# Two banded attentions: keys projected once per pair, the second half of the queries projected among the first attention units

## The reference

```
qkv = x @ w_qkv + b_qkv             # 16 query heads, 4 key and 4 value heads, 64 wide
# blocks of 128 queries; block n sees the keys of blocks n-1 and n
scores = einsum('bnqhgd,bnkhd->bnhgqk', q, kb) * 64 ** -0.5
scores = where(band and has_prev, scores, -inf)
probs = softmax(concatenate([scores, sink]))[..., :-1]
out = einsum('bnhgqk,bnkhd->bnqhgd', probs, vb) @ w_o + b_o
```

## Time and profile before

| | us |
|---|---|
| median of three runs | 4046.59 |
| lowest, highest | 4042.22, 4052.07 |
| the profiled execution, its own time | 4044.99 |
| its span in the trace | 4043.2 |
| PE busy | 3593.7 (89%) |
| DVE, ACT busy | 1854.7 (46%), 1375.2 (34%) |
| mean granted clock of PE | 0.914 |

### The profile page before, as it was taken

How to read it: one execution, slowest core, us unless ns; L and a number is a source line. 1 busy time by engine, 2 the same in 40 slices (tenths; PEclk the granted TensorE clock), 3 DMA queues, 4 the chain that set the end, 5 groups by cost and what they waited for, 6 DMA issues and landing times.

```text
span 4043.2 us, 47237 instructions
## 1 busy us (share of the span) xinstructions
PE 3593.7 (89%) x20284; PEld 2936.8 (73%) x20284; DVE 1854.7 (46%) x2920; ACT 1375.2 (34%) x2362; POOL 127.6 (3%) x167
## 2 busy tenths in 40 slices
PE   7988989885898989668798999997998999799898
PEld 6976979754697966367597987795555788656697
DVE  4524555404455544543455542553334555603476
ACT  3423444411344432110244432441342443312354
POOL 0000000000000000011000000001001000000000
PEclk9987999997899989676798997998999999899999
DMA  6542545435454523621454542541002233422253
GB/s 223 189 120 73 188 152 188 138 123 180 136 188 151 185 83 125 198 84 63 139 185 151 188 145 70 167 157 54 26 24 83 92 116 136 135 84 73 79 180 107
DMA packets 421534, 523.45 MB, mean 129 GB/s; under 512 B 53927, under 2 KB 363804, under 8 KB 421196
## 3 DMA queue, kind: packets, MB, share of 16 engines
q1 hardware_dynamic: 420524, 518.33, 39.3%
q0 software_dynamic: 800, 2.10, 0.2%
HBM read 518.29 MB, written 2.10 MB: 129 GB/s over the span
## 4 chain that ended last, share of the span: by engine, by line
PE 84%; DVE 9%; ACT 4%; POOL 2%; issue 1%; DMA 1%; SPq 0%; POOLq 0%; DVEq 0%; ACTq 0%
PE ps L184 17%; PE ps L185 17%; PE ps L186 16%; PE ps L176 15%; PE ps L194 3%; PE ps L272 3%; PE ps L947 3%; PE ps L404 1%; PE ps L1496 1%; PE ps L1123 1%; POOL small L453 1%; PE ps L2572 1%; PE ps L1266 1%; POOL junk L2308 1%; ACT junk L494 1%
## 5 line engine op out<-in xcount | busy, mean ns | idle before, releaser
L184 PE MATMUL ps<-a 128*128 128x256 f32 (+1 forms) x4488 | 1426.9, 318 | 53.8 <-DVE a L543 35.0
L185 PE MATMUL ps<-a 128*128 128x256 f32 (+1 forms) x4488 | 1423.9, 317 | 0.0
L186 PE MATMUL ps<-a 128*128 128x256 f32 (+1 forms) x4488 | 1420.8, 317 | 0.0
L184 PEld LDWEIGHTS ps<-a 128*128 128x128 f32 x4488 | 866.8, 193 | 116.6 <-issue 22.1
L186 PEld LDWEIGHTS ps<-a 128*128 128x128 f32 x4488 | 865.6, 193 | 54.4
L185 PEld LDWEIGHTS ps<-a 128*128 128x128 f32 x4488 | 867.0, 193 | 51.7
L674 DVE TENSOR_TENSOR a<-ring,a 128x1024 fp32r<-128x1024 f32 x594 | 693.6, 1222 | 371.1 <-ACT a L668 371.1
L668 ACT ACTIVATE a<-ring 128x1024 fp32r<-128x1024 f32 x594 | 585.9, 1048 | 280.7 <-PE ps L186 226.3
L765 ACT ACTIVATE tmp<-ps 128x256 f32<-128x256 f32 x176 | 67.6, 384 | 518.2 <-PE ps L186 518.2
L771 DVE TENSOR_TENSOR a<-tmp,ps 128x256 f32<-128x256 f32 x176 | 74.3, 422 | 309.4 <-ACT tmp L765 309.4
L176 PE MATMUL ps<-ring,xt 128*128 128x512 f32 (+1 forms) x512 | 207.4, 566 | 4.3 <-ACT xt L1057 2.9
(11 more groups left out here) (324 smaller groups left out, 3337.8 us busy)
## 6 DMA issues: line engine op xcount, KB each, us to landing
ring<-in_ffn_w_in_dram SPq DMA_DIRECT2D x220, 1024.0 KB, 7.3
ring<-in_ffn_w_out_dram SPq DMA_DIRECT2D x121, 1024.0 KB, 5.0
ring<-in_ada_w_dram SPq DMA_DIRECT2D x48, 1024.0 KB, 6.0
ring<-in_gla_w_in_dram SPq DMA_DIRECT2D x12, 1024.0 KB, 5.5
ring<-in_rwkv_w_rkv_dram SPq DMA_DIRECT2D x12, 1024.0 KB, 5.0
ring<-in_na_w_qkv_dram SPq DMA_DIRECT2D x12, 1024.0 KB, 5.1
ring<-in_swa_w_qkv_dram SPq DMA_DIRECT2D x10, 1024.0 KB, 5.1
ring<-in_swa_w_o_dram SPq DMA_DIRECT2D x8, 1024.0 KB, 5.0
```

What stands on the lines that cost most here:

```text
L184: pe.x.matmul(out, lh, rh, start=start and i == 0, stop=False)
L185: pe.x.matmul(out, lh, rl, start=False, stop=False)
L186: ins = pe.x.matmul(out, ll, rh, start=False, stop=stop and i == n - 1)
```

## The change

In both banded mixers:

- **Keys.** Two key blocks instead of four: block p holds key heads 2p and 2p+1, each once, from one 1 MB load. ACT evacuates each head with its bias into its own half of the partitions; the other half is filled by a DMA from SBUF to SBUF, four in all, issued by POOL and counted by a new semaphore `s_dup`. PE waits for all four before the first scores.
- **Order of the projections.** Keys, values, then query blocks 0 to 3, over banks 5, 6 and 7. Query blocks 4 to 7 are projected from the function `before`: PE computes block 3+i ahead of the scores of iteration i = 1 to 4, all into bank 5; ACT evacuates block 2+i ahead of its iteration i = 2 to 5. PE waits for the last of them ahead of iteration 6.
- **Order of the jobs.** First half of the heads for query blocks 0 and 1 (units 0, 1 and 2 to 5), then the second half (units 6, 7 and 8 to 11), since query blocks 4 to 7 hold the second half. The sinks' and the output's indices follow.
- **Transposes** use two banks (3 and 4) in turn here instead of three; the other attentions keep three.

```diff
 def pe_attention(...):                        # and the same in act_attention
-            if m >= 3:
-                pe.wait_ge(*s.act.at(tag, "pt", m - 3))
-            flips(K, pe, K.ps[:, 3 + m % 3, :], ...)
+            if m >= A.turns:
+                pe.wait_ge(*s.act.at(tag, "pt", m - A.turns))
+            flips(K, pe, K.ps[:, 3 + m % A.turns, :], ...)
 def swa_memory(K, tag, layer, j):
-    for t in range(2):
-        for half in range(2):
+    for half in range(2):
+        for t in range(2):
 def sp_swa(K, sp, M, f):
+    load_cols(K, sp, (tag, "k"), w, 1024, 256, 8, (s.pe, (tag, "k", 1)))
+    sp_projB(K, sp, (tag, "v"), w, 1280, 256, (0, 1))
     sp_projA(K, sp, (tag, "q"), w, 0, D)
-    for g0 in (0, 2):
-        c = K.w.take((tag, "k", g0), 4, (K.s.pe, (tag, "k", g0 + 1)))
...
-    sp_projB(K, sp, (tag, "v"), w, 1280, 256, (0, 1))
+def pe_swa_queries(K, pe, M, i, rot):
+    c = K.w[(tag, "q"), i // 2 * 256]
+    bank, freed = rot.take(s.act, tag, "q", "out", i)
+    pe.wait_ge(*c.landed)
+    pe.wait_ge(*freed)
+    mms(pe, bank[:, 0:T], [...8 pairs...]).then_inc(*s.pe.up((tag, "q"), i))
 def pe_swa(K, pe, M, f):
-    rot = Turns(K, range(6))
-    pe_projA(K, pe, (tag, "q"), D, xt, T, rot, s.act)
-    for g in range(4):
+    rot = Turns(K, (5, 6, 7))
+    for p in range(2):
...
     pe_projB(K, pe, (tag, "v"), 256, xt, (0, 1), rot, lambda i: s.dve)
-    pe.wait_ge(*s.act.at((tag, "k"), "out", 3))
+    for i in range(4):
+        pe_swa_queries(K, pe, M, i, rot)
     pe.wait_ge(*s.dve.at((tag, "v"), "out", 1, 0))
+    pe.wait_ge(*s.act.at(tag, "q", "out", 3))
+    pe.wait_ge(K.s_dup, 64 * (M.j + 1))
+    last = Turns(K, (5,))
+    def before(K, pe, i):
+        if 1 <= i <= 4:
+            pe_swa_queries(K, pe, M, 3 + i, last)
+        if i == 6:
+            pe.wait_ge(*s.act.at(tag, "q", "out", 7))
 def act_swa(K, act, M, f):
+    for p in range(2):
+        act.wait_ge(*s.pe.at(tag, "k", p))
+        for n in range(2):
+            g, half = 2 * p + n, slice(n * 64, n * 64 + 64)
+            ins = act.x.activation(M.KT[half, g, :], ...[half, 0:T], AF.Identity, bias=...)
+    for i in range(4):
+        act_swa_queries(K, act, M, i)
+    def before(K, act, i):
+        if 2 <= i <= 5:
+            act_swa_queries(K, act, M, 2 + i)
 def pool_swa(K, pool, M, f):
+    for g in range(4):
+        pool.wait_ge(*s.act.at(tag, "k", "out", g // 2))
+        a, b = ...                            # the half that holds head g, and the other
+        pool.x.dma_start(M.KT[b, g, :], M.KT[a, g, :]).then_inc(K.s_dup, 16)
```

More of the change, by code:

```diff
@@ L934, in pe_attention @@
             pe.wait_ge(*s.act.at(tag, "e", m))
-            if m >= 3:
-                pe.wait_ge(*s.act.at(tag, "pt", m - 3))
-            flips(K, pe, K.ps[:, 3 + m % 3, :], [A.P[m % 3][:, tk(b)] for b in range(4)]).then_inc(*s.pe.up(tag, "flip", m))
+            if m >= A.turns:
+                pe.wait_ge(*s.act.at(tag, "pt", m - A.turns))
+            flips(K, pe, K.ps[:, 3 + m % A.turns, :], [A.P[m % 3][:, tk(b)] for b in range(4)]).then_inc(*s.pe.up(tag, "flip", m))
         if 0 <= i - 3 < n:
@@ L1024, with __init__ @@
 class Attention:
-    def __init__(self, K, tag, units, scale, mask=None, sink=None):
+    def __init__(self, K, tag, units, scale, mask=None, sink=None, turns=3):
+        self.turns = turns
         self.tag, self.units, self.scale, self.mask = tag, units, scale, mask
@@ L1129, in values, with act_swa_queries @@
         return M.V[:, b, kv * 64:(kv + 1) * 64]
-    pe_attention(K, pe, M.A, scores, values)
+    pe_attention(K, pe, M.A, scores, values, before)
     for t in range(2):
-        pe.wait_ge(*s.dve.at(tag, "o", 2 * t + 1))
+        pe.wait_ge(*s.dve.at(tag, "o", 2 + t))
         pe_turn(K, pe, tag, M.O[:, t, :], (2 * t, 2 * t + 1), t)
     pe_mixer_end(K, pe, tag, M.ot, f)
+def act_swa_queries(K, act, M, i):
+    s, tag = K.s, M.tag
+    act.wait_ge(*s.pe.at((tag, "q"), i))
+    act.x.activation(M.QT[:, i, :], K.place[tag, "q", "out", i][:, 0:T], AF.Identity, bias=K.col("swa_b%d" % M.j, i, 1)).then_inc(
+        *s.act.up(tag, "q", "out", i))
 def act_swa(K, act, M, f):
@@ L1140, in act_swa @@
     meet(K, act, ("f", f - 1))
-    for i in range(8):
-        act.wait_ge(*s.pe.at((tag, "q"), i))
-        act.x.activation(M.QT[:, i, :], K.place[(tag, "q"), "out", i][:, 0:T], AF.Identity, bias=K.col("swa_b%d" % M.j, i, 1)).then_inc(
-            *s.act.up((tag, "q"), "out", i))
-    for g in range(4):
-        act.wait_ge(*s.pe.at(tag, "k", g))
-        act.x.activation(M.KT[:, g, :], K.place[(tag, "k"), "out", g][:, 0:T], AF.Identity, bias=K.col("swa_b%d" % M.j, 8 + g, 1)).then_inc(
-            *s.act.up((tag, "k"), "out", g))
-    act_attention(K, act, M.A)
+    for p in range(2):
+        act.wait_ge(*s.pe.at(tag, "k", p))
+        for n in range(2):
+            g, half = 2 * p + n, slice(n * 64, n * 64 + 64)
+            ins = act.x.activation(M.KT[half, g, :], K.place[tag, "k", "out", p][half, 0:T], AF.Identity,
+                                   bias=K.col("swa_b%d" % M.j, 8 + g, 1)[half])
+            ins.then_inc(*(s.act.up(tag, "k", "out", p) if n else s.act.up()))
+    for i in range(4):
[3 more added lines that the diff above has]
+            act_swa_queries(K, act, M, 2 + i)
+    act_attention(K, act, M.A, before)
     for t in range(2):
```

35 lines of the change are left out of this document (17 added, 18 removed).

## The result

The changed kernel took 4064.2 us (median of six runs, 4058.5 to 4067.5) beside 4049.3 us for the kernel before (six runs, 4039.4 to 4054.9): ratio 1.0039, 95% interval 1.0023 to 1.0056. Forecast was 4049 with a range to 4062. The stretch from first scores to turn came out nearly as worked out; the sum over the program did not. The profiled execution took 4063.1 us with a span of 4061.2, 18.1 us more than before, and its mean granted clock is 0.911 against 0.914.

The account below looks back on a forecast made before the run. TensorE at half clock was taken to bound the banded attention's units. Per mixer 77.0 - 54.7 - 20.7 = +1.6 us, twice +3.2, gave 4048.2 against the profiled 4044.99; with 1.6 for the median 4049.8, say 4049; range 4028 to 4062.

Parts of the forecast that it names:

- First scores, keys, copies, table: Banded mixers' projections: six blocks fewer, first scores 20.7 us earlier, near 265.7; key copies cost no wait; no table reloads expected.
- rival C: Evacuation with bias inside the exponentials reloads ACT's table in each of three waits: +7.7 us per mixer, 4065; chance 0.04.
- The chained waits: Moved query blocks wait on bank 5's evacuation behind exponentials: PE gaps of 4.1, 3.6, 2.7 us before q5 to q7.
- B: Clock does not come back in the moved query blocks, each lasting 6.9 us: +11 us per mixer, 4069; chance 0.10.
- D: Waits before the moved query blocks are shorter than chained, blocks hidden as meant: -9.4 us per mixer, 4028; chance 0.05.
- deciding step: Return of query blocks 4 to 7 among the units: first scores to turn 77.0 us, wrong if under 73 or over 81.
- Normalization, then half clock: At the units' first normalization PE stands about 2.6 us, the clock falls and stays at 0.50 until the turn.
- Units: First scores to turn in each banded mixer: 38.2 + 38.8 = 77.0 us, against 54.7 before.
- Turn and output: Banded mixer's end after the units: the turn expected near 343; no change of time entered in the sum.
- The sum: Whole kernel: 77.0 - 54.7 - 20.7 = +1.6 us per mixer, +3.2 in all, say 4049 us, no change that can be told.
- The range: Whole kernel's time 4028 to 4062 us, taking in gains on one side and reaching toward table reloads on the other.

Follow-up runs that it names:

- Experiment 3: Changed kernel with the moved query blocks alternating between banks 7 and 5 instead of all in bank 5; 4021.63 us, ratio 0.9956 to the kernel before.
- experiment 5: Changed kernel, single bank kept, with only the sinks' exponential taken early, at the job's last unit; 4043.84 us, ratio 1.0003 to the kernel before.
- experiment 6: Changed kernel with query blocks 4 to 7 back in the projections, early sinks' exponential, eight unread multiplications before unit 2's scores; 4032.38 us, ratio 0.9970 to before.
- experiment 13: Also written x8: changed kernel plus 16 unread multiplications (32 PE records) in the first mixer's end; median 4067.5 us, ratio 1.0029 to before.
- x10: Kernel before plus 48 unread multiplications (96 PE records) in the first banded mixer's end; ratio 1.0028 to the kernel before.
- experiment 4: Changed kernel with two banks for the moved query blocks and the sinks' exponential at the job's last unit; 4005.11 us, ratio 0.9916 to before.

## Why the prediction was wrong

- **First scores, keys, copies, table**: right. 266.19 against 265.7; both phases together gave 41.4 us, as forecast (2 x 20.7). No wait for the copies, no reload (rival C out).
- **The chained waits**: right. 3.95, 3.37, 2.44 us for 4.1, 3.6, 2.7; q5 to q7 6.17, 5.38, 5.41 us for the 5.4 taken; rivals B and D out. Experiment 3 shows the chain through the one bank to be the cause. By the prediction's own test (under 73 or over 81 us from first scores to turn) its deciding step held.
- **Normalization, then half clock**: right in what happened (2.03 us, then 0.50 to the turn), and with this wait gone the fall came 17 us later in one mixer and 3.5 us later in the other (experiment 5). The general reason given, that a gap of 2.48 us is enough and is what decides, falls with experiment 6: without it the clock fell 7 us later.
- **Units**: 78.1 and 77.7 for 77.0: 1.8 us more over both.
- **Turn and output**: taken as unchanged, 2.0 us longer each, 4.1 in all. The clock came back only at 352.7 us, in the output multiplication; before it was back at 345.1, behind the turn. In the second trace of after it was back at 346.7 us, and turn and output took 43.85 us, 0.9 less than before's 44.71. The term was left out; its size is between -0.9 and +2.0 us a mixer. So the mixers cost 9.1 us in the first pair of traces and 3.6 in the second. That 3.6 is so near to the forecast 3.2 is in part luck: the units were 2.0 us too long over both mixers, turn and output 1.7 too short.
- **The sum**: the step that failed. It added +3.2 us of the mixers to an otherwise fixed 4044.99, with nothing for turn and output and nothing for the stages without an edit; the medians differ by 14.9 us. The program around them isn't fixed: RWKV took 7.55 us more in the first pair of traces, and putting the 32 missing records back on PE gave this back (10.3 us in the one trace of experiment 13); the traces say that these records move an instruction fetch out of a transfer that PE waits for. In the second pair RWKV was equal (544.9 and 545.1), and the 11.2 us of difference were 3.6 in the mixers, 4.6 in the latent attention and 3.0 in the rest. Over all traces of this study the latent attention, never edited, takes 381.5 to 389.3 us; the cause of that was not tested. How the 14.9 us between the medians divide among these terms stays open, since most executions have no trace.
- **The range**: it held the bounds of the edited stages alone. With ±8 us for what edit-free stages do (they moved by 9.0 and 7.6 us in the two pairs) it would have reached past 4064.

## What to carry over

Work that is moved between units to fill a wait needed a second bank here: with one, each block is chained to the evacuation of the last, 78.1 against 60.2 us. Take small side steps, such as the sinks' exponential, out of the moment where PE waits: with both, the change is worth 0.8% where as written it costs 0.4%. And a forecast for a change under half a per cent in a kernel like this one, with 20 thousand records on PE, needs a range for stages it doesn't touch (8 to 9 us here), since those moved with the fetches of instructions and the changes of the clock.

## What the runs showed of the hardware

- A 16 KB fetch of PE's instructions in the midst of a 512 KB transfer went with a landing 1.5 us later (8.2 for 6.7), in 7 of 7 traces, and the later landing went with a shorter stage: the clock then was 1.00 and not 0.80 in a stretch of 61 us some 70 us later, and the stage was 7.5 us shorter in the first pair of traces.
- A multiplication of 128x128 by one column took 3.63 / 32 = 0.11 us a record at full clock (x8, at 378.95 us) and 15.9 / 96 = 0.17 us in x10, where the clock fell to half after 5 us; unread work was free within the idle 7 us (x8) and not beyond it (x10).
- One instruction stream (experiment 4) ran its units at 1.00 in one mixer and fell to 0.50 after 32 us in the other, and two further traces of the same units did the same.
